# Trunk kernel: 96 columns of the gated input made beside the rotary keys, and the spatial product placed behind the first two scores

## The chip, the cores and the metric

The program runs on one core of one Trainium2 chip. The metric is the device time of one execution in microseconds. The five engines of the core are TensorE (PE), VectorE (DVE), ScalarE (ACT), GpSimd (POOL) and SyncE (SP); SP only issues transfers here.

## The reference

A first block (a context pass, a two-dimensional Fourier mix, gated delta attention and a mixture of 32 experts) hands x (256 tokens, 1024 channels) to two late layers. Each late layer begins with an attention part, and the change lies there:

```python
h = rms_norm(x, mix_pre_g[l])
proj = h @ w_in[l]
cq, ckv, kr, z, dq, dk, dv = jnp.split(proj, IN_SPLIT, axis=-1)
out_a = mla_group(cq, ckv, kr, ...)
out_b = sgu_group(z, ...)
out_c = diff_group(dq, dk, dv, ...)
mix = jnp.concatenate([out_a, out_b, out_c], axis=-1) @ w_mix_out[l]
```

The widths are cq 384, ckv 256, kr 32 (the rotary part of the keys), z 512, and dq, dk, dv 256 each. The gated part is

```python
z = jax.nn.gelu(z, approximate=True)
u, v = jnp.split(z, 2, axis=-1)
v = layer_norm(v.reshape(b, nc, SGU_CHUNK, SGU_GROUPS, SGU_GROUP_DIM), g_sgu)
mixed = jnp.einsum('gts,bnsgc->bntgc', w_s, v) + b_s.T[:, :, None]
return (u * mixed).reshape(b, s, SGU_WIDTH)
```

diff_group takes two softmaxes per head (4 heads, 32 channels each) and subtracts one from the other; mla_group has 8 heads. Behind the attention come a cross attention on a memory and a convolutional feed-forward layer. All of it is computed in float32.

## The kernel before, in words

All weights come through one stream of 1 MB slots (`stream`), which SP moves into a ring of slots in SBUF in the order in which PE uses them. The host lays the stream out. For `w_in` it pads the 1952 columns to 2048: columns 0 to 671 hold cq, ckv and kr, columns 672 to 767 are zeros, and z, dq, dk, dv follow from 768. The padded matrix is cut into eight slots of 256 columns.

The order on each engine is written out by hand, one function per engine, and semaphores tie them. In a late layer PE (`mm`, line 716, issues every product; L714 is the same helper's transpose) does this at the head of the layer:

- three slots with `late_a` and `seven` for cq and ckv (channels on partitions; `seven` is a seven-product form of a 2x2 block product whose parts DVE joins), and from the second half of the third slot `late_b(s, h, range(TT), P, 32)`: the 32 rotary key columns, for both tiles of 128 tokens, 16 products (line 1496). `late_b` puts tokens on partitions, with h as the stationary operand and weight columns as the moving one.
- three slots with `seven` for dq, dk, dv, with the sums of squares of cq and ckv between them;
- two slots with `late_b(s, h, range(TT), 0, T)`, 256 columns each (line 1505): first v, the half of z that is normalized, then u, the half that gates;
- the spatial product of `sguw` and v into PSUM bank 2 (16 f32 records), `turn(0)` and `turn(1)`, which transpose dq and dk, and `scores(0)` and `scores(1)` (lines 1615 to 1626);
- the query projections `job_q`, then `turn_p(0)`, which transposes the first head's probabilities. Before it waits for them it issues seven products that nobody reads (`idle_products`).

ACT takes each product out of PSUM (`late_take` waits for PE, `late_out` copies or applies a function and reports to `late_ev`, line 2158). For the head it copies cq, ckv and kr, squares them, takes roots, applies gelu to v (`zt[:, :, T:2 * T]`), takes the root for the layer norm of v once DVE has its sums, applies gelu to u (`zt[:, :, 0:T]`), and then copies the turned dq and dk for the scores (`turned_in`, line 2261). gelu lies in another function table than ln and exp, so a table load stands before each gelu and behind it (`roots_table`).

DVE joins the `seven` products, rotates kr, dq and dk (`qk_ok`), normalizes v (`ln_ok`), and then takes `maxima(0)`, `maxima(1)`, `gating` (the spatial product plus its bias, times u) and `normalize(0)`, in this order.

Of the kernel before, what the change touches and what calls it, by code (L numbers as in the profile page):

```python
# [15 lines left out]
ACT = mybir.ActivationFunctionType  # L16
AX = mybir.AxisListType

P = 128
D = 1024  # L20
T = 256
TT = T // P
# [24 lines left out]
Y_SUMS, Y_AT = 18, {"win": 0, "mix": 4, "q": 8, "mem": 10, "ffn": 14}  # L47
QUADS = PAIRS // 2
XSLOTS = 3
KV_START, KV_MIX, KV_GAP = 4, 2, (1, 2, 1)  # L50


# [67 lines left out]
def trunk_kernel(nc, stream, par_d, row_d, cst_d, dft_d, xc_d, mem_d, pos_d, sguw_d, out_d):  # L120
    ctx = ExitStack()
    with ctx:
# [193 lines left out]
        h = xm  # L316
# [10 lines left out]
        krt = A(9984, TT, 32)  # L327
        zt = A(10048, TT, 512)
# [73 lines left out]
        qk_ok, tq_ps, tq_ev = sem("qk_ok"), sem("tq_ps"), sem("tq_ev")  # L402
# [302 lines left out]
        def _(pe):  # L705
# [179 lines left out]
            s = arrive()  # L885
# [15 lines left out]
            s = arrive()  # L901
# [14 lines left out]
            s = arrive()  # L916
# [14 lines left out]
            s = arrive()  # L931
# [442 lines left out]
            def late_b(s, src, toks, lo, n, kc=KC, width=None, within=None):  # L1374

                b = late_bank()
                for i, t in enumerate(toks):
                    for c in range(kc):
                        if within and c == 2:
                            within()  # L1380
                        last = c == kc - 1
                        mm(bank(b, len(toks) * n)[:, i * n:i * n + n], src[:, c, t * P:t * P + P],
                           wB(s, c, lo, n, kc, width), c == 0, last,
                           late_ps if last and i == len(toks) - 1 else None)
# [96 lines left out]
            for l in range(LAYERS):  # L1481
# [5 lines left out]
                for k in range(3):  # L1487
                    s = arrive()
                    if k == 1:
                        seven(4, s, h, hs2, ws[0], sums_at(l, "win", 2), y_sum)  # L1490
                        release()
                        continue
                    for half in range(2 if k < 2 else 1):
                        late_a(s, half, h, h0 if k == 0 and half == 0 else None)
                    if k == 2:
                        late_b(s, h, range(TT), P, 32)
                    release()
                for k in range(5):
                    s = arrive()
                    if k < 3:  # L1500
                        if k:
                            pe.wait_ge(cb_ok, joins_at(l, "win", k))
                        seven((6, 4, 6)[k], s, h, hs2, ws[(1, 0, 1)[k]], sums_at(l, "win", 3 + k), y_sum, True)
                    else:
                        late_b(s, h, range(TT), 0, T)
                    release()
                    if k == 0:
                        pe.wait_ge(cq_ok, l + 1)
                        for lo, hi in ((0, 3), (3, 5)):
                            for c in range(lo, hi):  # L1510
                                mm(bank(3, 2, T)[:, lo // 3, :], ones, sq[:, c, :], c == lo, c == hi - 1,
                                   cs_ps if c == 4 else None)
# [9 lines left out]
                def turn(k):  # L1522

                    if k >= 4:
                        pe.wait_ge(tq_ev, tq0 + k - 3)
                    b = 4 + k % 4
                    if k < 2:
                        for c in range(2):
                            for t in range(TT):
                                mm(bank(b, 2, T)[:, c, t * P:t * P + P],  # L1530
                                   dt_[:, t, k * 256 + c * P:k * 256 + c * P + P], ident, tr=True,
                                   inc=tq_ps if c and t else None)
                    else:
                        src = qt if k < 6 else kc
                        for hh in range(2):
                            hd = 2 * ((k - 2) % 4) + hh
                            for t in range(TT):
                                mm(bank(b, 2, T)[0:MLA_D, hh, t * P:t * P + P],
                                   src[:, t, hd * MLA_D:hd * MLA_D + MLA_D], ident, tr=True,
                                   inc=tq_ps if hh and t else None)  # L1540

                def scores(u):

                    g = 16 * l + u
                    if u < 4:
                        if u >= 2:
                            pe.wait_ge(exp_ok, g - 1)
                        for c in range(2):
                            for t in range(TT):
                                r = 64 * (u % 2) + 32 * c  # L1550
                                mm(bank(6 - 2 * (u % 2) + c, TT, T)[:, t, :], dqT[r:r + 32, u // 2, t * P:t * P + P],
                                   dkT[r:r + 32, u // 2, :], inc=sc_ps if c and t else None)
                    elif u < 12:
                        if u >= 8:
                            pe.wait_ge(exp_ok, g - 3)
                        for t in range(TT):
                            mm(bank(4 + u % 4, TT, T)[:, t, :], QT[0:MLA_D, u - 4, t * P:t * P + P],
                               KT[0:MLA_D, u - 4, :], inc=sc_ps if t else None)
                    else:
                        if u in (13, 14):  # L1560
                            pe.wait_ge(cb_ok, joins_at(l, "q", u - 12))
                        else:
                            pe.wait_ge(late_ev, q0 + 2 * (u // 15) + 2)
                        for t in range(TT):
                            for dc in range(2):
                                mm(bank(4 + u % 4, TT, T)[:, t, :], qm[:, 2 * (u - 12) + dc, t * P:t * P + P],
                                   (km0, km)[l][:, 2 * (u - 12) + dc, :], dc == 0, dc == 1, inc=sc_ps if t and dc else None)
# [38 lines left out]
                def turn_out(k):  # L1606
# [3 lines left out]
                    for c in range(2):  # L1610
                        for t in range(TT):
                            mm(bank(b, 2, T)[:, c, t * P:t * P + P], (ob, ot)[k][:, t, c * P:c * P + P], ident, tr=True,
                               inc=late_ps if c and t else None)

                pe.wait_ge(ld_sgu, 16 * (l + 1))
                pe.wait_ge(ln_ok, 3 * l + 2)
                for t in range(TT):
                    for g in range(4):
                        mm(bank(2, TT * 4, 64)[:, 4 * t + g, :], sguw[:, g, :], zt[:, t, 256 + 64 * g:256 + 64 * g + 64],
                           inc=mix_ps if t and g == 3 else None)  # L1620
                pe.wait_ge(qk_ok, 2 * l + 1)
                turn(0)
                turn(1)
                pe.wait_ge(tq_ev, tq0 + 2)
                scores(0)
                scores(1)
                pe.wait_ge(cv_ok, l + 1)
                s = arrive()
                job_q(s, 0)
# [171 lines left out]
        def _(act):  # L1801
# [355 lines left out]
            def late_out(dst, src, fn=ACT.Copy):  # L2157
                A_(dst, src, fn).then_inc(late_ev, 1)
# [72 lines left out]
            for l in range(LAYERS):  # L2231
# [5 lines left out]
                    b = late_take()  # L2237
                    late_out(cv[:, j, :], bank(b, T))
                b = late_take()
                late_out(krt, bank(b, TT, 32))  # L2240
                act.wait_ge(late_ev, ljobs[0] - 1)
                act.wait_ge(cb_ok, joins_at(l, "win", 1))
                A_(sq[:, 0:5, :], cv, ACT.Square).then_inc(cq_ok, 1)
# [6 lines left out]
                act.wait_ge(ln_ok, 3 * l + 1)  # L2250
                inverse_root(st8b, st8b, 64).then_inc(sm_ok, 1)
                b = late_take()
                late_out(zt[:, :, 0:T], bank(b, TT, T), ACT.Gelu_apprx_tanh)
                roots_table()

                def turned_in(k):
# [1004 lines left out]
```

## Time and profile before

| | us |
|---|---|
| median of 3 runs | 1720.34 |
| lowest and highest run | 1720.14, 1721.66 |
| the profiled execution, its own time | 1721.44 |
| its span, first to last instruction | 1718.7 |
| mean granted TensorE clock (1 is 2.4 GHz) | 0.994 |
| busy DVE, ACT, POOL | 935.4, 414.1, 187.1 |

The profile is of one execution. Its rows give a start in microseconds from the start of the span, a duration, the engine, the line of the kernel, and the operation with its tiles. A PE row in a timeline merges neighbours of the same kind, of which it shows the first one's shape; an entry in brackets is the idle time before the row and who ended it. A busy PE is not a PE at its peak, since its records overlap.

### The profile page before, as it was taken

The page shows a single profiled execution, that of the slowest core. Times are in us where ns is not written, and L with a number is a line of the kernel's source. Part 1 is how long each engine was busy: PE and PEld are TensorE (multiplying, and loading weights), DVE is VectorE, ACT ScalarE, POOL GpSimd, SP SyncE. Part 2 cuts the span into 40 slices and gives each one's busy share as a digit, 9 for nine tenths or more (in the row PEclk, how much of TensorE's full clock was granted, in tenths as well). Part 3 has the DMA queues.
Part 4 walks back from the last instruction along what each step waited for, and adds up shares of the span by engine and source line. Part 5 has one row for each costly group of instructions (what it writes and reads, how often), then busy time and mean ns, then how long its engine had stood idle before and what let it go on. Part 6 is the DMA issues. An engine that isn't in the chain of part 4 may idle for free.

```text
span 1718.7 us, 29906 instructions
## 1 busy us (share of the span) xinstructions
PE 1658.0 (96%) x12332; PEld 1358.9 (79%) x12332; DVE 935.4 (54%) x1997; ACT 414.1 (24%) x916; POOL 187.1 (11%) x144
## 2 busy tenths in 40 slices
PE   7999999999999999999999999999999999999997
PEld 4677787666666566567977989999989688999997
DVE  4899435122312312325455446999664644599985
ACT  3653321110011011012163322222022632322211
POOL 1021002100000000000000003232110000033231
PEclk9999999999999999999999999999999999999999
DMA  9311675799999999996432334444444223244420
GB/s 395 141 65 60 256 301 227 283 421 422 422 422 422 422 421 422 423 421 269 148 123 74 123 114 137 169 171 172 172 148 153 74 99 123 99 169 164 164 94 25
DMA packets 53671, 383.61 MB, mean 223 GB/s; under 512 B 6080, under 2 KB 6336, under 8 KB 7360
## 3 DMA queue, kind: packets, MB, share of 16 engines
q1 hardware_dynamic: 52272, 376.90, 56.0%
q10 hardware_dynamic: 1296, 5.24, 0.8%
q8 instruction: 76, 1.25, 0.3%
q14 instruction: 27, 0.22, 0.0%
HBM read 381.07 MB, written 1.05 MB: 222 GB/s over the span
## 4 chain that ended last, share of the span: by engine, by line
PE 87%; DMA 7%; DVE 2%; ACT 2%; issue 1%; SPq 0%; ACTq 0%; DVEq 0%
PE ps L716 83%; DMA ring<-in_stream 7%; PE ps L714 2%; PE ps L773 1%; DVE arena L2408 1%; DMA xT<-in_xc 1%; ACT arena L2272 0%; DVE small L2988 0%; DVE arena L2411 0%; DVE arena L2414 0%; ACT arena L2264 0%; ACT arena L2279 0%; DVE small L2408 0%; ACT arena L1923 0%; DVE xT L2408 0%
## 5 line engine op out<-in xcount | busy, mean ns | idle before, releaser
L716 PE MATMUL ps<-ring,arena 128*64 128x256 f32 (+5 forms) x3168 | 482.2, 416 | 14.1 <-DMA ring<-in_stream 11.1
L716 PE MATMUL ps<-arena,ring 128*128 128x128 f32 (+2 forms) x2768 | 486.1, 329 | 4.6 <-DVE arena L2414 1.1
L716 PEld LDWEIGHTS ps<-arena,ring 128*128 128x128 f32 x2768 | 405.5, 191 | 60.2 <-issue 32.2
L716 PE MATMUL ps<-arena 128*128 128x128 f32 (+5 forms) x3434 | 441.2, 287 | 7.8 <-DVE arena L2819 2.8
L716 PEld LDWEIGHTS ps<-ring,arena 128*64 128x64 f32 (+1 forms) x3168 | 292.7, 150 | 181.4 <-issue 102.0
L716 PEld LDWEIGHTS ps<-arena 128*128 128x128 f32 (+3 forms) x3434 | 405.5, 190 | 31.8 <-issue 17.6
L2408 DVE TENSOR_TENSOR arena<-arena,ps 128x256 f32<-128x256 f32 (+2 forms) x288 | 110.3, 403 | 234.1 <-ACT arena L2139 227.1
L583 POOL TENSOR_TENSOR arena<-arena 128x512 f32<-128x512 f32 x32 | 45.3, 1416 | 1059.4 <-ACT arena L2202 900.0
L2414 DVE SCALAR_TENSOR_TENSOR arena<-arena,par 128x255 f32<-128x255 f32 (+1 forms) x282 | 125.5, 487 | 4.1
L2819 DVE COPY arena<-ps 32x512 f32<-32x512 f32 x128 | 87.9, 687 | 60.2 <-PE ps L716 58.9
L2408 DVE TENSOR_TENSOR arena<-arena 128x256 f32<-128x256 f32 (+2 forms) x120 | 70.9, 607 | 73.0 <-ACT arena L1844 30.4
L583 POOL TENSOR_TENSOR arena<-ring 128x512 f32<-128x512 f32 x62 | 90.2, 1459 | 118.8 <-PE ps L716 93.2
L716 PE MATMUL ps<-extra,arena 128*128 128x128 f32 (+2 forms) x672 | 93.5, 285 | 0.0
L716 PEld LDWEIGHTS ps<-extra,arena 128*128 128x128 f32 (+1 forms) x672 | 83.1, 189 | 1.9
L2888 DVE COPY arena<-ps 128x128 f32<-128x128 f32 x68 | 19.7, 289 | 119.2 <-PE ps L716 119.2
L2408 DVE TENSOR_TENSOR arena<-arena,ring 128x512 f32<-128x512 f32 x82 | 75.6, 922 | 2.1
L2408 DVE TENSOR_TENSOR arena<-ring 128x512 f32<-128x512 f32 x102 | 76.1, 746 | 0.8
L2384 ACT ACTIVATE arena<-arena,par 128x256 f32<-128x256 f32 x80 | 43.7, 593 | 115.8 <-DVE arena L2408 115.8
L714 PE MATMUL ps<-cst,arena 128*128 128x128 f32 (+1 forms) x384 | 55.0, 275 | 8.3 <-DVE arena L2411 5.8
L2408 DVE TENSOR_TENSOR arena<-ring,arena 128x512 f32<-128x512 f32 x82 | 60.5, 738 | 2.7
L2139 ACT ACTIVATE arena<-ps 128x512 f32<-128x512 f32 x16 | 9.6, 597 | 210.8 <-PE ps L716 210.8
L714 PEld LDWEIGHTS ps<-cst,arena 128*128 128x128 f32 (+1 forms) x384 | 44.1, 142 | 15.1 <-ACT arena L2279 10.7
(211 smaller groups left out, 1171.7 us busy)
## 6 DMA issues: line engine op xcount, KB each, us to landing
ring<-in_stream SPq DMA_DIRECT2D x347, 1024.0 KB, 15.9
arena<-in_stream SPq DMA_DIRECT2D x9, 1024.0 KB, 19.4
extra<-in_stream SPq DMA_DIRECT2D x2, 1024.0 KB, 24.3
arena<-in_xc ACTq DMA_DIRECT2D x1, 1024.0 KB, 6.2
xT<-in_xc ACTq DMA_DIRECT2D x1, 1024.0 KB, 10.7
arena<-in_mem ACTq DMA_DIRECT2D x1, 1024.0 KB, 4.8
out_y<-xT ACTq DMA_DIRECT2D x2, 512.0 KB, 2.6
ring<-in_dft ACTq DMA_DIRECT2D x1, 512.0 KB, 8.0
```

What stands on the lines that cost most here:

```text
L583: return nc.gpsimd.tensor_tensor(out, a, b, op)
L714: i = nc.tensor.transpose(out, lhsT, rhs)
L716: i = nc.tensor.matmul(out, lhsT, rhs, start=start, stop=stop, skip_group_check=skip)
L773: mi = nc.tensor.matmul(mod_at(i)[q:q + 32, 0:T], silu_c[:, c, :], wB(s, c, 0, T), start=c < 4, stop=c >= 4, tile_position=(0, q))
L2139: A_(sg, bank(2, 512), ACT.Silu).then_inc(sg_ok, 1)
L2384: a = A_(ca[:, q, k, :], cb[:, q, k, :] if i else bank(2 + k // 2, 2, T)[:, k % 2, :], ACT.Identity, bias=PR(f"fbias{l}")[:, ch:ch + 1], s ...
L2408: return V.tensor_tensor(out, a, b, op)
L2414: return V.scalar_tensor_tensor(out, a, s1, b, op0, op1)
L2819: ins = V.tensor_copy(ytok[to:to + TSLOT, t, 512 * o:512 * o + 512], bank(2 + o, 512)[lo:lo + TSLOT, :])
L2888: link(V.tensor_copy(first_p[:, w], m[:, 0, :]))
```

## The change

In the second half of the third slot the 96 zero columns are replaced by the first 96 columns of u. The rotary product becomes 128 columns wide and carries them. The slot of u then holds the other 160 columns, and its product becomes 160 wide. ACT copies the early 96 columns from PSUM into `zt` before it copies kr, applies gelu to them there when the rest of u has come, and to the 160 columns straight from PSUM. On PE the spatial product is moved from before `turn(0)` to behind `scores(1)`.

```diff
+U_EARLY = P - 32
...
                     if k == 2:
-                        late_b(s, h, range(TT), P, 32)
+                        late_b(s, h, range(TT), P, P)
...
                     else:
-                        late_b(s, h, range(TT), 0, T)
+                        late_b(s, h, range(TT), 0, T if k == 3 else T - U_EARLY)
...
+                pe.wait_ge(qk_ok, 2 * l + 1)
+                turn(0)
+                turn(1)
+                pe.wait_ge(tq_ev, tq0 + 2)
+                scores(0)
+                scores(1)
                 pe.wait_ge(ld_sgu, 16 * (l + 1))
                 pe.wait_ge(ln_ok, 3 * l + 2)
                 for t in range(TT):
                     for g in range(4):
                         mm(bank(2, TT * 4, 64)[:, 4 * t + g, :], sguw[:, g, :], zt[:, t, 256 + 64 * g:256 + 64 * g + 64],
                            inc=mix_ps if t and g == 3 else None)
-                pe.wait_ge(qk_ok, 2 * l + 1)
-                turn(0)
-                turn(1)
-                pe.wait_ge(tq_ev, tq0 + 2)
-                scores(0)
-                scores(1)
                 pe.wait_ge(cv_ok, l + 1)
...
                 b = late_take()
-                late_out(krt, bank(b, TT, 32))
+                A_(zt[:, :, 0:U_EARLY], bank(b, TT, P)[:, :, 32:P], ACT.Copy)
+                late_out(krt, bank(b, TT, P)[:, :, 0:32])
...
                 b = late_take()
-                late_out(zt[:, :, 0:T], bank(b, TT, T), ACT.Gelu_apprx_tanh)
+                A_(zt[:, :, 0:U_EARLY], zt[:, :, 0:U_EARLY], ACT.Gelu_apprx_tanh)
+                late_out(zt[:, :, U_EARLY:T], bank(b, TT, T - U_EARLY), ACT.Gelu_apprx_tanh)
                 roots_table()
...
-        wp[:, :672] = w[:, :672]
-        wp[:, 768:] = w[:, 672:]
+        wp[:, :672 + U_EARLY] = w[:, :672 + U_EARLY]
+        wp[:, 768:1024 - U_EARLY] = w[:, 672 + U_EARLY:928]
+        wp[:, 1024:] = w[:, 928:]
```

PE in layer 0, the rotary product, before:

```order
L716 MATMUL ps<-ring,arena 128x32 [waits late_ev]
L716 MATMUL ps<-ring,arena 128x32 x15
L716 MATMUL ps<-ring,arena 128x128 [waits slot_full_late5]
L716 MATMUL ps<-ring,arena 128x128 x7
L716 MATMUL ps<-ring,arena 128x128 [waits ffn_sums]
```

and in the changed kernel (where lines are numbered one to three higher):

```order
L717 MATMUL ps<-ring,arena 128x128 [waits late_ev]
L717 MATMUL ps<-ring,arena 128x128 x15
L717 MATMUL ps<-ring,arena 128x128 [waits slot_full_late5]
L717 MATMUL ps<-ring,arena 128x128 x7
L717 MATMUL ps<-ring,arena 128x128 [waits ffn_sums]
```

The place and the wait are the same, and so is the `seven` product behind it; only the width changes.

PE in layer 0, from the two tiles of gated input to the first query projection, before:

```order
L716 MATMUL ps<-ring,arena 128x256 [waits late_ev,slot_full_late8]
L716 MATMUL ps<-ring,arena 128x256 x15
L716 MATMUL ps<-ring,arena 128x256 [waits late_ev,slot_full_late0]
L716 MATMUL ps<-ring,arena 128x256 x15
L716 MATMUL ps<-arena 128x64 [waits ln_ok,ld_sgu]
L716 MATMUL ps<-arena 128x64 x7
L714 MATMUL ps<-cst,arena 128x128 [waits qk_ok]
L714 MATMUL ps<-cst,arena 128x128 x7
L716 MATMUL ps<-arena 128x256 [waits tq_ev]
L716 MATMUL ps<-arena 128x256 x7
L716 MATMUL ps<-ring,arena 128x384 [waits late_ev,slot_full_late1,cv_ok]
```

and in the changed kernel:

```order
L717 MATMUL ps<-ring,arena 128x256 [waits late_ev,slot_full_late8]
L717 MATMUL ps<-ring,arena 128x256 x15
L717 MATMUL ps<-ring,arena 128x160 [waits late_ev,slot_full_late0]
L717 MATMUL ps<-ring,arena 128x160 x15
L715 MATMUL ps<-cst,arena 128x128 [waits qk_ok]
L715 MATMUL ps<-cst,arena 128x128 x7
L717 MATMUL ps<-arena 128x256 [waits tq_ev]
L717 MATMUL ps<-arena 128x256 x7
L717 MATMUL ps<-arena 128x64 [waits ln_ok,ld_sgu]
L717 MATMUL ps<-arena 128x64 x7
L717 MATMUL ps<-ring,arena 128x384 [waits late_ev,slot_full_late1,cv_ok]
```

The L714 and L715 rows are `turn(0)` and `turn(1)`, the 128x64 rows the spatial product, the rows that wait for `tq_ev` the scores. The spatial product has moved behind the scores, and the second tile is 160 wide.

ACT in layer 0, from the root of the layer norm to the copies of the turned tiles, before:

```order
L1843 ACTIVATE small<-small 128x8 [waits ln_ok]
L1844 ACTIVATE small<-small 128x8 [waits a_step]
L2158 ACT_TABLE_LOAD
L2158 ACTIVATE arena<-ps 128x2x256 [waits late_ps]
L1839 ACT_TABLE_LOAD
L2261 ACTIVATE arena<-ps 128x512 [waits tq_ps] x2
```

and in the changed kernel:

```order
L1844 ACTIVATE small<-small 128x8 [waits ln_ok]
L1845 ACTIVATE small<-small 128x8 [waits a_step]
L2255 ACT_TABLE_LOAD
L2255 ACTIVATE arena<-arena 128x2x96 [waits late_ps]
L2159 ACTIVATE arena<-ps 128x2x160
L1840 ACT_TABLE_LOAD
L2264 ACTIVATE arena<-ps 128x512 [waits tq_ps] x2
```

One activation of 512 elements has become two, of 192 and 320, between the same two table loads. One more copy, of 128x2x96 elements, stands ahead of the copy of kr. DVE, POOL and SP issue the same instructions as before.

## Rows read from the trace of the kernel before

**Rows 1.** The page, busy us of each engine (share of the span) xinstructions.

```profile
PE 1658.0 (96%) x12332; PEld 1358.9 (79%) x12332; DVE 935.4 (54%) x1997; ACT 414.1 (24%) x916; POOL 187.1 (11%) x144
```

**Rows 2.** Timeline, layer 0, rotary product: start us, us, engine, line, operation, tiles.

```profile
824.90 8.04 PE L716 MATMUL ps<-ring,arena 128*128 128x32 f32 x56
825.11 0.38 ACT L2158 ACTIVATE arena<-ps 128x256 f32<-128x256 f32 x1 [9.32 <-PE ps L716]
...
828.60 0.22 ACT L2158 ACTIVATE arena<-ps 128x64 f32<-128x64 f32 x1 [3.11 <-PE ps L716]
828.95 1.27 ACT L2243 ACTIVATE arena<-arena 128x1280 f32<-128x1280 f32 x1
...
832.78 3.74 PE L716 MATMUL ps<-arena 128*128 128x128 f32 x32
```

**Rows 3.** Timeline, layer 1, the same place.

```profile
1288.16 6.41 PE L716 MATMUL ps<-ring,arena 128*128 128x32 f32 x56
1288.36 0.38 ACT L2158 ACTIVATE arena<-ps 128x256 f32<-128x256 f32 x1 [9.32 <-PE ps L716]
...
1291.85 0.23 ACT L2158 ACTIVATE arena<-ps 128x64 f32<-128x64 f32 x1 [3.11 <-PE ps L716]
...
1294.41 3.74 PE L716 MATMUL ps<-arena 128*128 128x128 f32 x32
```

**Rows 4.** Windows: stretch, length, PE busy (records), granted clock, DMA share, GB/s.

```profile
596.70:600.10 3.40, 3.40 (x20) 0.50 1.01 422
782.70:786.00 3.30, 3.30 (x30) 1.00 1.01 422
828.80:832.40 3.60, 3.60 (x20) 0.53 0.56 221
1291.80:1295.20 3.40, 3.40 (x33) 1.00 0.49 161
```

**Rows 5.** Timeline, layer 0, from the gated input to the first softmax.

```profile
851.02 13.98 PE L716 MATMUL ps<-ring,arena 128*128 128x256 f32 x64
...
862.17 0.21 ACT L1844 ACTIVATE small<-small 128x8 f32<-128x8 f32 x1
862.40 1.28 ACT L2158 ACT_TABLE_LOAD   x1
...
864.84 1.89 PE L716 MATMUL ps<-arena 128*128 128x64 f32 x16
865.04 0.60 ACT L2158 ACTIVATE arena<-ps 128x512 f32<-128x512 f32 x1 [1.36 <-PE ps L716]
865.65 1.28 ACT L1839 ACT_TABLE_LOAD   x1
...
866.57 1.04 PE L714 MATMUL ps<-cst,arena 128*128 128x128 f32 x8
867.21 1.09 ACT L2261 ACTIVATE arena<-ps 128x512 f32<-128x512 f32 x2 [0.27 <-PE ps L714]
...
868.35 1.17 PE L716 MATMUL ps<-arena 32*128 32x256 f32 x16 [0.74 <-ACT arena L2261]
...
869.45 4.14 PE L716 MATMUL ps<-ring,arena 128*128 128x384 f32 x12
...
872.28 0.74 DVE L2408 TENSOR_TENSOR arena<-ps,par 128x256 f32<-128x256 f32 x2
...
873.42 1.72 PE L716 MATMUL ps<-cst 128*128 128x128 f32 x14
...
874.92 0.88 DVE L2414 SCALAR_TENSOR_TENSOR arena<-arena,small 128x256 f32<-128x256 f32 x2
...
875.86 0.66 PE L714 MATMUL ps<-cst,arena 128*128 128x128 f32 x4 [0.71 <-DVE arena L2414]
```

**Rows 6.** Timeline of PE: two of its five waits between 2.2 and 2.8 us.

```profile
595.91 8.81 PE L716 MATMUL ps<-ring,arena 128*64 128x256 f32 x64 [2.49 <-DMA ring<-in_stream]
...
782.63 3.83 PE L716 MATMUL ps<-arena 128*128 128x128 f32 x32 [2.77 <-DVE arena L2819]
```

## The prediction

> **What bounds the kernel now.** I read the page's busy shares first: TensorE (PE) is busy for 1658.0 us, 96% of the span, and the chain that ended last is mostly its own work [rows 1]. So an edit is worth what it takes out of PE's time or out of one of PE's waits, and both must be read in the stretch that is touched. That is the head of each of the two late layers. I read layer 0 there in the timeline; layer 1 repeats the same pieces. Each f32 product stands in the trace as two MATMUL records. Then I read the granted clock in the windows view, because one group of records had a strange length, and last PE's longest waits.
>
> The head of layer 0 runs like this [rows 5]. PE makes the two tiles of gated input, 64 records from 851.02 to 864.84, 216 ns each. Then come the spatial product (16 records, 864.84 to 866.57, 1.73 us), the eight transposes of turn 0 and 1 (to 867.6, 1.04 us), and a wait of 0.74 us for ACT, which copies the turned queries and keys out of PSUM. The first two scores take 868.35 to 869.45, two query projections 869.45 to 873.42, the seven idle products from 873.42 to 875.0 (14 records of 112 ns). Then PE waits for the first softmax (DVE and ACT) until 875.86. What the reader is to see is who is late at the two waits: ACT before the scores, and DVE before turn_p(0), the transposes of the first probabilities. The last DVE pieces before 875.86 are in [rows 5].
>
> **Part 1: the rotary product, 32 columns to 128.** In both layers ACT's copies around it stand 3.49 us apart (825.11 to 828.60, 1288.36 to 1291.85), so its 32 records take 109 ns each [rows 2, 3]. The 24 records of 128 columns behind it in layer 1 take 2.56 us (1291.85 to 1294.41), 107 ns each, and all 56 together 112 ns each from the first one's start to the next product's (1288.16 to 1294.41) [rows 3]. Four times the columns cost the same here, since each record brings a weight load of its own. I cost the wider product at 0, between -0.1 and +0.1 us per layer.
>
> The strange length is in layer 0: the same 24 records behind the product take 828.60 to 832.78, 4.18 us [rows 2]. That is 1.62 us more than in layer 1. The windows say why: from 828.8 to 832.4 the mean granted clock is 0.53 (it is at its lower level, 1.2 GHz, nearly throughout), and in the same place of layer 1 it is 1.00, that is 2.4 GHz [rows 4]. What the engine did before it fell is 3.5 us of records only 32 columns wide. With 128 columns it streams four times as much in the same time, as in the products around it, behind which the clock stays up. So I expect this low spell to go: -1.62 us in this execution, nothing in layer 1, where it did not come. Bounds: 0 (the spell had another reason) and -1.62 for each layer that had one.
>
> The added copy on ACT (2x96 columns) comes before the copy of the rotary keys. From 64 columns at 0.22, 256 at 0.38 and 512 at 0.60 us [rows 2, 5] I take 0.33 us. It delays the squares, which ACT starts at 828.95 and PE needs only after 832.78 + 3.5 = 836.3 [rows 2]; they take 1.3 us, so 6 us of PE's work cover it. If that cover were gone it would cost its 0.33 us.
>
> **Part 2: the last tile, 256 to 160 columns.** 32 records of 216 ns become 32 of something between 112 ns (128 columns) and 216 ns (256). No row has 160; a line between these two gives 138 ns. The tile then takes 4.4 instead of 6.9 us: 2.5 us of PE work go in each layer, bounds 0 and 3.3. But this is not the gain, for PE meets the ACT wait earlier.
>
> **Part 3: ACT before the scores.** ACT ends its table load at 862.40 + 1.28 = 863.68 and then waits 1.36 us for the tile until 865.04 [rows 5]. In the new kernel the tile is ready at about 862.5, so ACT goes on at 863.70: the activation of the early 2x96 columns (0.33 us) and of the 2x160 (0.44), a table load (1.28) to 865.8, then the two copies of turned tiles (1.09), which now find their PSUM tile long ready. Scores start at 866.94 instead of 868.35: 1.4 us earlier. Bounds: 0.9 (if both small activations cost 0.6 each) and 1.4.
>
> The page "ScalarE: Activation LUTs" of the Trainium skill, section What ACT_TABLE_LOAD costs, adds a drain of about 1.38 us to each load of 1.28 us. By that rule ACT could not have gone on at 863.70, the 1.36 us wait would be this drain, and the sum below would be that of the third rival. The row behind the second load speaks against it: that load ends at 866.93, and ACT's next copy starts at 867.21, released by PE [rows 5].
>
> **Part 4: the order on PE.** The spatial product moves behind the scores. PE is through with tile and turns at 851.02 + 6.91 + 4.4 + 1.04 = 863.4 and now waits about 3.6 us for ACT, against 0.74 before: most of the 2.5 us saved, and the moved 1.73 us, turn into this wait. From the scores on it runs 866.94 + 1.10 (scores) + 1.73 (spatial) + 3.97 (queries) + 1.57 (idle products) = 875.3. The softmax side comes with its scores, 1.4 us earlier: 874.45. DVE's gating, which needs the spatial product and starts at 872.28 behind the second maxima [rows 5], would start at 870.9; the product is ready at 870.0, so this wait costs nothing with 0.9 us of cover. DVE has normalize(0) queued behind the gating, and PE waits for that. So turn_p(0) starts at the later of 875.3 and 874.45. PE itself is now last, and the wait of 0.71 us for DVE goes. **Gain 0.55 us per layer, 1.1 us in both**, bounds 0.1 and 0.55. Behind it PE works without a long gap, ACT and DVE follow its products, so the 0.55 us is carried along. No DMA is added; the weight slots of two tiles come free up to 3 us earlier on a queue that is not late here.
>
> **Part 5: the clock in the new wait.** 3.6 us is longer than any PE wait but the first one of the program. Five waits for DMA or DVE lasted 2.26 to 2.77 us. After the one before 595.91 (2.49 us) the clock was at 0.50 from 596.7 to 600.1; after the one before 782.63 (2.77 us) it stayed at 1.00 [rows 4, 6]. Two of the five had a low spell. So I expect one here more often than not: chance 0.7 in a layer. A spell costs at most what [rows 2, 3] show, 1.62 us, and part of it lies within the wait, where it costs nothing. I take 1.2 us when it comes, 0.9 us per layer on average, 1.8 us in both; bounds 0 and 3.2. It lands on PE's own chain, which has just become the last.
> The page "TensorE: Matmul & The Clock Gate" of the Trainium skill, section Why this matters for your kernels, tells one to avoid long idle gaps between bursts of matmuls, as the engine then falls back to its lower clock. By that rule both layers would pay and the sum would be 0.6 us higher. The trace agrees in two of five cases only.
>
> **Sum.** The profiled execution took 1721.44 us (span 1718.7): -1.62 - 1.1 + 1.8 gives 1720.5. The median of the runs is 1720.34, 1.1 us lower, and the runs lie 1.5 us apart, about one low spell. So I count only half of the 1.62 against the median: 1720.34 - 0.8 - 1.1 + 1.8 = 1720.2 us. A measurement of this kernel can tell about 0.2% (3.4 us) from no change; this is far inside.
>
> **Rivals.**
> 1. *The clock holds in the new wait.* Then nothing is given back: 1720.34 - 0.8 - 1.1 = 1718.4, and 1717.6 if the median had a full spell to lose; with one in each layer even 1716.0. For it: three of five waits. Against it: this wait is 0.8 us longer than all of them. Chance 0.20.
> 2. *Slower: the clock falls in the wait before the scores and stays down past the query projections.* The gap is followed by scores on 32 rows and a product of 64 columns, narrow work like that of Part 1, so a second spell may follow at once. Two spells on the chain are 3.2 us per layer, less 0.55: 1720.34 - 0.8 + 5.3 = 1724.8. It decides from the point where low-clock work costs over 0.55 us in a layer (break-even), and over 2.7 us per layer it leaves the 0.2%. Against it: one spell was all that followed the 2.49 us wait. Chance 0.06.
> 3. *ACT is not earlier* (a drain after its load, or 160 columns that cost like 256). Scores start at 868.35 + 0.2 for the second small activation, and with the spatial product behind them turn_p(0) starts at 868.5 + 8.4 = 876.9, 1.0 us later than now: 1720.34 - 0.8 + 2.0 = 1721.6. Against it: the 0.28 us behind the second load, and the records of 128 columns at 112 ns. Chance 0.10.
>
> **How the numbers follow.** The forecast, "half a microsecond won in each layer and a low spell exchanged for another", has 0.64: 1720.2 us, its own range 1718.6 to 1721.9. Range of all: 1717.4 (most of rival 1) to 1722.6 (rival 3, and four spells instead of two). Faster than 1716.9 needs a spell gone from both layers and none in the waits, or a gain that I do not see: 0.09. Slower than 1723.8 is rival 2 and something unseen: 0.07. Within 0.2%: 0.84.
>
> **What would show it.** Part 1: at full clock behind the rotary product in both layers, 24 records in 2.56 us, the product itself 3.5 us. Part 2: 32 records of 160 columns in about 4.4 us. Part 3: no wait of ACT before the early activation, scores 1.4 us after it would be otherwise. Part 4: a PE wait of about 3.6 us for ACT before the scores, none of DVE's 0.71 us before turn_p(0), and from the first gated tile to turn_p(0) 24.3 us instead of 875.86 - 851.02 = 24.84. Part 5: windows at 0.5 behind the wait. I am wrong if the wait before the scores is under 2 us, if turn_p(0) still waits for DVE, or if the time leaves 1717.4 to 1722.6.

## The result and the profile after

| | before | change |
|---|---|---|
| median of 20 runs, us | 1720.87 | 1725.2 |
| lowest and highest run, us | 1718.86, 1728.74 | 1722.52, 1731.15 |
| ratio to before, 95% interval | | 1.0024 [1.0017, 1.0031] |
| profiled execution (span), us | 1721.44 (1718.7) | 1728.73 (1726.8) |
| mean granted clock of the profiled execution | 0.994 | 0.988 |

The change makes the kernel slower: the medians are 4.3 us apart, and the ratio (0.24%) is clear of 1 by its interval. The forecast was 1720.2 us within 1717.4 to 1722.6; the time is outside, on the side of rival 2.

The page's first section of the changed kernel (busy us of each engine), which answers to [rows 1]:

```profile
PE 1662.0 (96%) x12332; PEld 1362.8 (79%) x12332; DVE 935.6 (54%) x1997; ACT 415.0 (24%) x920; POOL 187.1 (11%) x144
```

PE is 4.0 us busier in a kernel from which some 5 us of PE work were taken. The timeline of layer 0 shows where (start us, us, engine, line, operation; it answers to [rows 2] and [rows 5]):

```profile
828.16 6.41 PE L717 MATMUL ps<-ring,arena 128*128 128x128 f32 x56
...
831.93 0.33 ACT L2241 ACTIVATE arena<-ps 128x192 f32<-128x192 f32 x1 [3.19 <-PE ps L717]
...
834.41 3.74 PE L717 MATMUL ps<-arena 128*128 128x128 f32 x32
...
852.65 11.42 PE L717 MATMUL ps<-ring,arena 128*128 128x256 f32 x64
...
863.90 1.04 PE L715 MATMUL ps<-cst,arena 128*128 128x128 f32 x8
864.02 1.28 ACT L2255 ACT_TABLE_LOAD   x1
...
865.32 0.36 ACT L2255 ACTIVATE arena<-arena 128x192 f32<-128x192 f32 x1
865.59 0.42 ACT L2159 ACTIVATE arena<-ps 128x320 f32<-128x320 f32 x1
...
868.46 5.72 PE L717 MATMUL ps<-arena 32*128 32x256 f32 x32 [3.52 <-ACT arena L2264]
...
873.97 5.92 PE L717 MATMUL ps<-ring,arena 128*128 128x384 f32 x12
874.21 0.76 DVE L2411 TENSOR_TENSOR arena<-ps,par 128x256 f32<-128x256 f32 x2 [0.78 <-PE ps L717]
...
876.86 0.88 DVE L2417 SCALAR_TENSOR_TENSOR arena<-arena,small 128x256 f32<-128x256 f32 x2
...
879.73 1.72 PE L717 MATMUL ps<-cst 128*128 128x128 f32 x14
...
881.29 0.60 PE L715 MATMUL ps<-cst,arena 128*128 128x128 f32 x4
```

Up to the scores all went as forecast. The rotary product and the 24 records behind it take 6.25 us (828.16 to 834.41), as in layer 1 before [rows 3]. The second tile is short: both tiles together take 11.25 us (852.65 to 863.90), so the 32 records of 160 columns take 4.34 us. ACT's table load ends at 865.30 and the next activation starts at 865.32, without a drain and without a wait. PE waits 3.52 us, and the scores start 15.81 us after the first gated tile, against 868.35 - 851.02 = 17.33 before: 1.5 us earlier. Then everything on PE is slow. Scores and spatial product take 5.51 us (868.46 to 873.97) instead of 2.83, the query projections 5.76 instead of 3.97. turn_p(0) starts at 881.29, 28.64 us after the first tile, against 24.84 before. The wait for DVE's last piece (876.86 + 0.88) has gone, and PE is late by more than 3 us of its own.

A spell is a stretch at the lower clock. The windows of PE behind the start of the scores (stretch, length, PE busy and records, granted clock, DMA share, GB/s), first three of layer 0, then three of layer 1:

```profile
868.40:871.80 3.40, 3.34 (x22) 0.50 0.00 0
871.80:875.20 3.40, 3.40 (x14) 0.50 0.00 0
875.20:877.40 2.20, 2.20 (x5) 0.50 0.00 0
1333.86:1335.00 1.14, 1.14 (x17) 1.00 0.06 22
1335.00:1336.00 1.00, 1.00 (x7) 0.52 0.00 0
1337.40:1341.00 3.60, 3.60 (x10) 0.50 0.00 0
```

In layer 0 the clock stays at its lower level of 1.2 GHz from within the wait to beyond 877. In layer 1 it falls only at about 1335, 1.1 us after the scores have begun, and stays low into the projections. PE's timeline of layer 1:

```profile
1318.05 11.42 PE L717 MATMUL ps<-ring,arena 128*128 128x256 f32 x64
...
1333.86 4.72 PE L717 MATMUL ps<-arena 32*128 32x256 f32 x32 [3.52 <-ACT arena L2264]
1338.37 5.83 PE L717 MATMUL ps<-ring,arena 128*128 128x384 f32 x12
...
1345.60 0.60 PE L715 MATMUL ps<-cst,arena 128*128 128x128 f32 x4
```

Here turn_p(0) starts 27.55 us after the first tile. The two heads are 3.80 and 2.71 us longer than before. The low spell behind the rotary product of layer 0 is gone (-1.62 us). One more spell stands behind a wait ahead of the late layers, where both kernels do the same. The profiles of e7, e8 and e11 have it too, the other nine do not. The product there took 3.83 us before [rows 6], and now

```profile
783.14 6.57 PE L717 MATMUL ps<-arena 128*128 128x128 f32 x32 [2.77 <-DVE arena L2822]
```

6.57 us, 2.7 more. By the time of the rotary product the profiled execution of the change is 3.26 us behind (828.16 against 824.90), most of it by this. The sum 3.26 - 1.62 + 3.80 + 2.71 = 8.15 us is the difference of the two spans, 8.1 us. What belongs to the change is 4.9 us of this, near the 4.3 us of the medians.

### The profile page after: what moved, and what is told of

Its sections match the earlier page's. It is cut to its first block, busy times and chain, and to the rows that moved or that the text cites. A ratio compares the mean times of both kernels' runs of the same rounds, so it can differ in the third digit from the quotient of the medians.

```text
span 1726.8 us, 29910 instructions
## 1 busy us (share of the span) xinstructions
PE 1662.0 (96%) x12332; PEld 1362.8 (79%) x12332; DVE 935.6 (54%) x1997; ACT 415.0 (24%) x920; POOL 187.1 (11%) x144
## 4 chain that ended last, share of the span: by engine, by line
PE 87%; DMA 7%; ACT 3%; DVE 2%; issue 1%; SPq 0%; ACTq 0%; DVEq 0%
PE ps L717 83%; DMA ring<-in_stream 7%; PE ps L715 2%; PE ps L774 1%; DVE arena L2411 1%; DMA xT<-in_xc 1%; ACT arena L2275 0%; ACT arena L2267 0%; DVE arena L2414 0%; ACT arena L2282 0%; DVE small L2411 0%; ACT arena L2159 0%; ACT arena L1924 0%; DVE xT L2411 0%; ACT L1840 0%
## 5 line engine op out<-in xcount | busy, mean ns | idle before, releaser
L717 PE MATMUL ps<-arena 128*128 128x128 f32 (+5 forms) x3434 | 448.2, 291 | 13.4 <-ACT arena L2264 7.0
L717 PEld LDWEIGHTS ps<-arena 128*128 128x128 f32 (+3 forms) x3434 | 411.8, 193 | 38.4 <-issue 18.6
L715 PE MATMUL ps<-cst,arena 128*128 128x128 f32 (+1 forms) x384 | 54.9, 275 | 6.9 <-DVE arena L2414 5.9
L715 PEld LDWEIGHTS ps<-cst,arena 128*128 128x128 f32 (+1 forms) x384 | 44.2, 141 | 13.4 <-ACT arena L2282 10.7
```

The source lines that it names most:

```text
L715: i = nc.tensor.transpose(out, lhsT, rhs)
L717: i = nc.tensor.matmul(out, lhsT, rhs, start=start, stop=stop, skip_group_check=skip)
```

## The experiments

**The theory**: the clock falls in the thin stretch from the turns over the 3.5 us wait to the spatial product and stays low, and all other parts of the change gain. **Rivals**: the narrow work behind the wait is to blame and not the wait; the order costs by itself; the widths and ACT's extra instructions cost.

| run | what | median us (lowest to highest, runs) | ratio to before, 95% interval |
|---|---|---|---|
| | the change | 1725.2 (1722.52 to 1731.15, 20) | 1.0024 [1.0017, 1.0031] |
| e1 | change, wait filled with 14 products | 1717.32 (1715.76 to 1718.92, 9) | 0.9978 [0.9969, 0.9988] |
| e2 | change, spatial product between turns and scores | 1717.6 (1715.04 to 1722.43, 10) | 0.9982 [0.9971, 0.9994] |
| e3 | widths only | 1720.81 (1715.68 to 1723.27, 12) | 0.9995 [0.9986, 1.0003] |
| e4 | order only | 1728.86 (1727.41 to 1730.25, 5) | 1.0047 [1.0034, 1.006] |
| e5 | e2, its two waits filled | 1716.16 (1714.35 to 1717.47, 6) | 0.9972 [0.996, 0.9984] |
| e6 | before, rotary product 128 wide | 1719.79 (1717.49 to 1725.15, 12) | 0.9996 [0.9985, 1.0006] |
| e7 | e1 with 32-column filler | 1720.74 (1717.67 to 1725.73, 11) | 0.9998 [0.999, 1.0007] |
| e8 | e1 with half the filler | 1723.41 (1717.7 to 1726.16, 12) | 1.0007 [0.9996, 1.0017] |
| e9 | e4, wait filled | 1723.4 (1720.64 to 1725.36, 11) | 1.0013 [1.0004, 1.0022] |
| e10 | e6, its wait before the scores filled | 1719.28 (1717.16 to 1722.29, 11) | 0.9985 [0.9974, 0.9995] |
| e11 | e7 again | 1719.98 (1717.71 to 1728.09, 11) | 1.0 [0.9989, 1.0011] |

The diffs of e1, e2 and e3 are against the change, those of e4 and e6 against the kernel before, those of e7 and e8 against e1, and the others as they say. The kernel before ran beside each group: medians 1720.94 (e1 to e4), 1720.62 (e5 to e8) and 1721.05 us (e9 to e11).

### e1: fill the wait

```diff
                 turn(0)
                 turn(1)
+                idle_products(3, 14)
                 pe.wait_ge(tq_ev, tq0 + 2)
```

> The change, with 14 unread products (28 records of 128 columns, 3.1 us) between the turns and the wait before the scores. Theory (the clock falls because PE idles 3.5 us there): no low spell in the windows behind the scores; the wait is about 0.4 us; turn_p(0) starts 24.3 us after the first gated tile; median near 1719.0, below the kernel before. Rival (the narrow work behind the wait, scores on 32 rows and the 64-column product, brings the clock down, and the wait has no part in it): the spells of 3.4 to 10 us stay and the median stays near 1725.

PE's timeline of layer 0, and two windows behind the start of the scores:

```profile
849.59 11.42 PE L717 MATMUL ps<-ring,arena 128*128 128x256 f32 x64
...
861.72 3.29 PE L717 MATMUL ps<-cst 128*128 128x128 f32 x28
865.39 3.10 PE L717 MATMUL ps<-arena 32*128 32x256 f32 x32 [0.39 <-ACT arena L2265]
868.33 4.09 PE L717 MATMUL ps<-ring,arena 128*128 128x384 f32 x12
...
873.81 0.60 PE L715 MATMUL ps<-cst,arena 128*128 128x128 f32 x4
```

```profile
865.40:868.80 3.40, 3.40 (x34) 1.00 0.02 5
868.80:872.20 3.40, 3.40 (x12) 1.00 0.00 0
```

The wait is 0.39 us, the clock full, scores and spatial product take 2.94 us and the projections 3.92. turn_p(0) starts 24.22 us after the first tile, in both layers. The median is 7.9 us under that of the change. 14 products whose results nobody reads are all that was added, so 7.9 us is what the low clock costs in the change; the two heads of the profiled executions give 4.42 + 3.33 = 7.75 us. The rival without a part for the wait falls. The median is also 1.7 us under the 1719.0 that I expected. The span shows where this comes from: it is 2.8 us under that of the kernel before, which is the whole spell behind the rotary product and both heads (1.62 + 2 x 0.62 = 2.86), and I had counted only half of that spell.

### e2: the spatial product between turns and scores

```diff
                 turn(0)
                 turn(1)
-                pe.wait_ge(tq_ev, tq0 + 2)
-                scores(0)
-                scores(1)
                 pe.wait_ge(ld_sgu, 16 * (l + 1))
...
+                pe.wait_ge(tq_ev, tq0 + 2)
+                scores(0)
+                scores(1)
                 pe.wait_ge(cv_ok, l + 1)
```

> The change, with the spatial product between the turns and the scores instead of behind the scores. Theory: the wait before the scores shrinks to about 1.2 us (with a short one before the spatial product), no low spell, and since nothing stands between scores and queries PE is not last: turn_p(0) comes 1.4 us earlier than before (23.4 us after the first gated tile), median near 1717.3. Rival (narrow work is the cause): the same narrow products stand there, still with a wait between them, so spells stay in part and the median is 1721 or more.

```profile
849.82 11.42 PE L717 MATMUL ps<-ring,arena 128*128 128x256 f32 x64
...
862.83 1.97 PE L717 MATMUL ps<-arena 128*128 128x64 f32 x16 [0.72 <-DVE arena L2411]
865.62 1.17 PE L717 MATMUL ps<-arena 32*128 32x256 f32 x16 [0.82 <-ACT arena L2264]
...
873.12 0.66 PE L715 MATMUL ps<-cst,arena 128*128 128x128 f32 x4 [0.70 <-DVE arena L2417]
```

The profiled execution is as forecast: waits of 0.72 and 0.82 us, turn_p(0) 23.30 us after the first tile, 1.54 earlier than before, with DVE last again (0.70 us). The median is as low as that of e1, but the runs spread over 7.4 us where those of e1 spread over 3.2. In four of the ten runs the time is 1720.1 us or more, and no trace shows where those lose it.

### e3: the widths only

```diff
+                pe.wait_ge(ld_sgu, 16 * (l + 1))
+                pe.wait_ge(ln_ok, 3 * l + 2)
+                for t in range(TT):
+                    for g in range(4):
...
                 pe.wait_ge(qk_ok, 2 * l + 1)
                 turn(0)
                 turn(1)
                 pe.wait_ge(tq_ev, tq0 + 2)
                 scores(0)
                 scores(1)
-                pe.wait_ge(ld_sgu, 16 * (l + 1))
-                pe.wait_ge(ln_ok, 3 * l + 2)
...
```

> Only the widths of the change (128 and 160 columns), PE's order as before. Theory: PE waits about 1.7 us before the spatial product for the layer norm and under 1 us before the scores; the scores come 0.8 us earlier than before, no low spell, turn_p(0) 24.0 us after the first gated tile, median near 1718.5. Rival (the widths themselves, by ACT's additional instructions, cost the time): median above 1722.

PE's timeline, layer 0 and then layer 1:

```profile
862.51 2.92 PE L717 MATMUL ps<-arena 128*128 128x64 f32 x16 [1.60 <-DVE arena L2411]
...
867.82 2.12 PE L717 MATMUL ps<-arena 32*128 32x256 f32 x16 [0.69 <-ACT arena L2264]
869.87 5.95 PE L717 MATMUL ps<-ring,arena 128*128 128x384 f32 x12
...
1313.93 11.42 PE L717 MATMUL ps<-ring,arena 128*128 128x256 f32 x64
1326.95 1.97 PE L717 MATMUL ps<-arena 128*128 128x64 f32 x16 [1.60 <-DVE arena L2411]
...
1338.03 0.66 PE L715 MATMUL ps<-cst,arena 128*128 128x128 f32 x4 [0.70 <-DVE arena L2417]
```

Layer 1 shows the full clock: turn_p(0) after 24.10 us. In layer 0 the same work is slow from the spatial product on (2.92 against 1.97 us, then 2.12 against 1.17, then 5.95 against 4.14), behind a wait of only 1.60 us. The widths give what was expected in one layer and lose it to the clock in the other, and the median of 1720.81 is the same as before. My expectation that waits of 1.6 and 0.7 us are short enough was wrong. The rival (ACT's additional instructions) has no support: layer 1 has them too and is 0.74 us shorter than before.

### e4: the order only

```diff
+                pe.wait_ge(qk_ok, 2 * l + 1)
+                turn(0)
+                turn(1)
+                pe.wait_ge(tq_ev, tq0 + 2)
+                scores(0)
+                scores(1)
                 pe.wait_ge(ld_sgu, 16 * (l + 1))
...
-                pe.wait_ge(qk_ok, 2 * l + 1)
-                turn(0)
-                turn(1)
-                pe.wait_ge(tq_ev, tq0 + 2)
-                scores(0)
-                scores(1)
```

> Only the order of the change, widths as before (32 and 256 columns). Theory: the wait before the scores is 2.2 us, so spells come in some layers and not in others; without a spell turn_p(0) is 0.6 us later than before, since the spatial product now stands between scores and queries on PE; median 1722 to 1723.5. Rival (narrow work behind the scores is the cause, whatever the wait): spells as long as in the change, median 1725 or more.

```profile
866.77 4.07 PE L716 MATMUL ps<-arena 32*128 32x256 f32 x32 [2.21 <-ACT arena L2261]
870.63 6.51 PE L716 MATMUL ps<-ring,arena 128*128 128x384 f32 x12
...
1332.32 5.24 PE L716 MATMUL ps<-arena 32*128 32x256 f32 x32 [2.21 <-ACT arena L2261]
```

A wait of 2.21 us brings a spell in both layers: scores and spatial product take 3.86 and 5.03 us instead of 2.83. All five runs lie between 1727.4 and 1730.3. The median is 5.4 us above the upper end of my 1722 to 1723.5. It came out as the rival had it, so the wait alone is not the measure: 2.77 us in front of wide products left the clock alone in the profile of before [rows 4, 6], 2.2 us between transposes and these narrow products did not in either layer.

### e8: half the filler

```diff
-                idle_products(3, 14)
+                idle_products(3, 7)
```

> e1 with 7 unread products instead of 14: PE waits about 2.0 us before the scores. Theory: spells come in some runs only; median between e1 (1717.3) and the change (1725), near 1721, and a spread of the runs wider than that of e1. Rival (any filler is enough): 1717.3.

```profile
867.14 4.88 PE L717 MATMUL ps<-arena 32*128 32x256 f32 x32 [1.95 <-ACT arena L2265]
...
1331.38 4.90 PE L717 MATMUL ps<-arena 32*128 32x256 f32 x32 [1.95 <-ACT arena L2265]
```

The wait is 1.95 us and both layers of the profiled execution have a spell (scores and spatial product 4.88 and 4.90 us, where e1 has 3.10). The median stands between those of e1 and the change, nearer to the change, and the spread is 8.5 us. The median is 2.4 us over my 1721; the rival (any filler is enough) falls.

### e7 and e11: a filler that is busy but narrow

```diff
-                idle_products(3, 14)
+                for _ in range(14):
+                    mm(bank(3, 32), ones, ident[:, 0:32])
```

> e1 with the 14 unread products 32 columns wide instead of 128. The wait is as full of records as in e1 (about 3.1 us, since a record costs 110 ns either way), only narrower. If idleness as such brings the clock down: no spells, 1717.3 as in e1. If it is too little streamed work, as behind the rotary product: spells come back in most runs, and the median is 1720 to 1724.

> e7 once more, since its one profile fell on an execution without a spell at the head. If the narrow filler lets the clock fall: the median is again 1720 to 1722, above e1, and this profile may show a window at 0.5 behind the scores in a layer. If e7's median was chance: 1717.3.

The profile of e7 fell on an execution of 1720.74 us, just its median, 3.0 us over the profiled execution of e1. It has no spell at either head: turn_p(0) starts 24.23 us after the first tile in layer 0 and 24.22 in layer 1, as in e1. The 3.0 us stand ahead of the late layers, for the most part in the row that the change had too, where e1 has 3.83 us:

```profile
783.02 6.62 PE L717 MATMUL ps<-arena 128*128 128x128 f32 x32 [2.77 <-DVE arena L2824]
```

e11 repeats e7, and its profile has a spell at the head of layer 0 and none in layer 1. Its timeline in layer 0, and three of its windows:

```profile
861.85 3.40 PE L717 MATMUL ps<-cst 128*128 128x32 f32 x28
865.53 5.72 PE L717 MATMUL ps<-arena 32*128 32x256 f32 x32 [0.28 <-ACT arena L2266]
871.04 6.04 PE L717 MATMUL ps<-ring,arena 128*128 128x384 f32 x12
```

```profile
864.00:865.00 1.00, 1.00 (x10) 0.86 0.98 418
865.00:866.00 1.00, 0.71 (x6) 0.50 0.57 238
868.00:872.00 4.00, 4.00 (x18) 0.50 0.02 4
```

The clock fell before 865, while PE was still in the narrow filler and before its 0.28 us of idle time. It stayed low for scores, spatial product and projections (11.39 us from 865.53 to 876.92 instead of 6.9 in e1). So a spell can begin here without any idle time before it. How often it does is less clear. One of the four heads in these two profiles has a spell. The intervals of both runs lie above that of e1, which differs in the width of the filler alone, but barely (0.999 and 0.9989 against an upper end of 0.9988), and the execution of e7 with the median time lost nothing at the head. That a narrow filler protects less than a wide one fits this, and is not settled.

### e6: the rotary product alone

```diff
-                        late_b(s, h, range(TT), P, 32)
+                        late_b(s, h, range(TT), P, P)
...
-                late_out(krt, bank(b, TT, 32))
+                late_out(krt, bank(b, TT, P)[:, :, 0:32])
```

> The kernel before, where only the rotary product streams 128 columns (the 96 of padding too). Theory (Part 1: the narrow product brought the clock down behind it): the product still takes 3.5 us, no low spell behind it in either layer, median 0.8 us lower than before, 1720.1. Rival (the spell there had another reason): no change, spells behind it still in some runs.

```profile
825.26 6.41 PE L716 MATMUL ps<-ring,arena 128*128 128x128 f32 x56
...
1286.88 6.42 PE L716 MATMUL ps<-ring,arena 128*128 128x128 f32 x56
```

The product costs nothing more at 128 columns (56 records take 6.4 us in both layers), and no spell stands behind it, here or in any of the other nine profiles with 128 columns. With 32 columns, layer 0 of all three profiles (before, e4 and e9) has the 8.04 us of [rows 2], and layer 1 of none. So the width decides here. The median is 0.8 us lower than before, as expected, but the interval takes in 1.

### e9: the price of the order without the clock

```diff
                 turn(0)
                 turn(1)
+                idle_products(3, 9)
                 pe.wait_ge(tq_ev, tq0 + 2)
```

(on top of e4)

> Only the order of the change (as e4, widths as before), with nine unread products (18 records, 2.0 us) in the 2.2 us wait before the scores. This prices Part 4 without the clock. Theory: no spell at the head, turn_p(0) 25.4 us after the first gated tile (24.84 + 0.58), because the spatial product stands between scores and queries; median 1720.6 + 1.2 = 1721.8, some 7 us under e4 (1728.9). Rival (the order itself costs several us): median above 1725.

```profile
849.93 13.98 PE L716 MATMUL ps<-ring,arena 128*128 128x256 f32 x64
...
867.00 3.10 PE L716 MATMUL ps<-arena 32*128 32x256 f32 x32 [0.20 <-ACT arena L2262]
...
875.42 0.60 PE L714 MATMUL ps<-cst,arena 128*128 128x128 f32 x4
```

turn_p(0) starts after 25.49 us, in both layers: the order alone costs 0.65 us per layer by the chain on PE, as worked out (0.58). The filler takes 5.5 us off e4's median, and that part was the clock. The median of e9 is 1.6 us higher than I expected. Its runs lie in three groups, near 1720.7, 1723.4 and 1725.2, and the profile fell on one of the lowest; what the others lost, and where, no trace shows.

### e5 and e10: filling the short waits

e5 is e2 with

```diff
                 turn(0)
                 turn(1)
+                idle_products(3, 3)
                 pe.wait_ge(ld_sgu, 16 * (l + 1))
...
+                idle_products(3, 3)
                 pe.wait_ge(tq_ev, tq0 + 2)
```

> The spatial product between turns and scores as in e2, with three unread products (6 records, 0.67 us) before it and three before the scores, which fill the two waits of 0.72 and 0.82 us. Theory (what PE leaves undone there brings the clock down): no low spell in any run, turn_p(0) still 23.3 us after the first gated tile with DVE last, so the median is 1.5 to 2 us under e2: near 1716. Rival (e1 is already all there is, and turn_p(0) waits for DVE in any case): the same 1717.5.

and e10 is e6 with the second of these insertions.

> The kernel before with the rotary product 128 columns wide (e6) and three unread products (0.67 us) in its wait of 0.74 us before the scores. Theory (the kernel before also had spells at this place in some runs, which would explain why e1 gains 3.5 us where 1.1 + 0.8 are accounted for): median 0.7 to 1.5 us under e6, 1718.5 to 1719. Rival (no spells there): 1719.8 as e6.

In the profile of e5 the clock is full at both heads, and turn_p(0) starts 23.31 us after the first tile with DVE last, as expected. e5 has the lowest median of all, 1716.16 us, 0.28% under the kernel before, and it is the version to keep. Its 1.4 us on e2 come with a spread of 3.1 instead of 7.4 us, but the intervals of e1, e2 and e5 overlap, so their order is not settled. e10 is 0.5 us under e6, less than the runs can tell: whether the kernel before now and then had a spell at its own wait of 0.74 us stays open.

## Why the prediction was wrong

- **Part 1** (rotary product free, its spell goes): right. 6.25 us for the 56 records; e6 shows it alone. The -0.8 us for the median agrees with e6 and is not resolved. All three profiles with 32 columns have the spell in layer 0, which speaks for the whole 1.62 us, where I counted half.
- **Part 2** (160 columns): right, 4.34 us against 4.4.
- **Part 3** (ACT 1.4 us earlier): right, 1.5 us. The early copy took 0.33 us, the two activations 0.36 and 0.42 us. The page "ScalarE: Activation LUTs" of the Trainium skill, section What ACT_TABLE_LOAD costs, has a drain behind a table load; the trace does not agree, with 0.02 us between the load and the next activation. Rival 3 fell with it.
- **Part 4** (0.55 us per layer gained, PE last instead of DVE, a wait of 3.6 us): right where the clock is full. e1 has 24.22 us against 24.84, and the wait was 3.52 us. In the change DVE's gating waited for the spatial product only because that product was slow (874.21, after 0.78 us); in e1 it does not wait.
- **Part 5** is the step that failed: "chance 0.7 in a layer", "1.2 us when it comes", "1.8 us in both; bounds 0 and 3.2". Measured: a spell in both layers of the profiled execution, and 7.9 us for both by the medians of the change and e1. The heads of 28.64 and 27.55 us are 4.4 and 3.3 us longer than the 24.22 of e1. (The 1.8 was also rounded up: 2 x 0.7 x 1.2 is 1.7.) I priced a spell by [rows 2, 3], where wide products followed it and it ended at once. I saw a reason why it might not end here, the narrow work behind the wait, and gave it 0.06 as rival 2. Its mechanism is what was measured, except that the clock came back within the query projections (a granted clock of 0.87 from 877.4 to 878.4) and not behind them. That its time (1724.8 us) is so near the measured 1725.2 is partly luck: it added 5.3 us for both heads, where the profiled execution has 3.80 + 2.71 = 6.5.
- Two errors lie under this. I counted the wait alone, 3.6 us against 2.26 to 2.77, though [rows 2] had just shown a spell without any wait. And I asked how often a wait is followed by a spell, and what it then costs, from one execution and from waits that stand in front of wide products. In the 13 profiles the same five waits have a spell behind them in 37 of 65 cases, the one before 782.63 in four of 13, and there it cost up to 2.8 us. In front of narrow products e4 has two spells of two behind 2.21 us, e3 one of two behind 1.60 us. The page "TensorE: Matmul & The Clock Gate" of the Trainium skill, section Why this matters for your kernels, warns of long idle gaps. The trace agrees for this change, with a low clock behind the wait in both layers; e11 shows a fall with the gap filled by narrow products.
- The sum without Part 5 was 1720.34 - 0.8 - 1.1 = 1718.4; e1, which is that sum, has 1717.3. With the whole 1.62 us for the rotary spell, as the spans of e1 and before bear out, it would be 1717.6.

## What to carry to other kernels

Before taking work off TensorE ahead of a wait, ask what becomes of the time: if the engine behind it is not earlier by as much, the saved work is an idle stretch, and the low clock that follows can cost more than the edit saves (here 7.9 us, against the 3.6 us by which e1 is under the kernel before). Judge such a stretch by all that is thin in it, the wait with the narrow products and transposes on both sides, and price a spell by the work that will follow it, not by a spell elsewhere. The remedy is to move useful work into the wait (e2), and to fill what is left with wide products that nobody reads (e1; e5 is not told apart from e2 by its interval).

## What the runs showed that I had not expected

- The clock can fall in a stretch without idle time: within the 28 records of 32 columns ahead of the scores it went from 1.00 to 0.50, between 864 and 865 us (e11).
- The clock does not come back during the scores and the spatial product. It was still 0.50 in the change at 877 us, more than 8 us after PE had resumed and 3 us into the wide query projections.
- A wait of 1.60 us was enough in one layer of e3, while 2.77 us in front of wide products did nothing in the profile of before [rows 6] and was followed by a slow stretch (6.57 us for the same product) in that of the change. Whether a spell comes differs between executions of one kernel; the spread of the runs (3.2 us in e1, 8.5 in e8) fits this, though only one execution of each kernel has a trace.
